# Two token blocks read by turns as TensorE's moving operand, in the expert scores and queries

## The reference, cut to what matters

```python
def peer_ffn(x, wq, sub_keys, u, v):
    q = jnp.einsum('bld,dk->blk', x, wq).reshape(b, L, PEER_HEADS, 2, PEER_HALF)
    s = jnp.einsum('blhpc,hpnc->blhpn', q, sub_keys)
    # two top-k steps choose eidx (which experts) and the gates g = softmax(top_s)
    def blk(inp):                       # one block of 128 tokens
        h = jnp.einsum('td,tkd->tk', xt, u[et])
        a = gt * jax.nn.gelu(h, approximate=False)
        return jnp.einsum('tk,tkd->td', a, v[et])
```

## Time and profile before

| | us |
|---|---|
| median of 3 executions | 3771.06 (3770.87 to 3773.51) |
| the profiled execution, its own time | 3770.78 |
| its span, first to last instruction | 3768.9 |
| TensorE busy in it | 3748.6 |
| VectorE busy | 2470.0 |
| ScalarE busy | 1904.0 |
| GpSimd busy | 974.0 |

### The profile page before, as it was taken

One profiled execution on the slowest core, in us unless ns is written; L12 is line 12 of the kernel. 1 busy time (PEld: TensorE's weight loads), 2 busy tenths in 40 slices (PEclk: granted clock), 3 DMA queues, 4 the chain that ended last, 5 costly groups with the idle time before them and its releaser, 6 DMA issues.

```text
span 3768.9 us, 58143 instructions
## 1 busy us (share of the span) xinstructions
PE 3748.6 (99%) x19216; PEld 3168.9 (84%) x19216; DVE 2470.0 (66%) x4281; ACT 1904.0 (51%) x2859; POOL 974.0 (26%) x557
## 2 busy tenths in 40 slices
PE   9999999999999999999999999999999999999998
PEld 7778888888888888888787788888888888888887
DVE  6766599985555555555687665999855555555556
ACT  4675455554444444444456654555544444444443
POOL 1000038777760000000011000477777600000000
PEclk9999999999999999999999999999999999999999
DMA  8665567777777666666666555677777776666664
GB/s 299 235 213 190 202 201 213 210 216 211 208 210 265 244 239 239 244 240 239 216 227 236 186 201 191 213 210 210 217 209 210 211 266 244 241 237 244 243 238 172
DMA packets 294652, 842.44 MB, mean 224 GB/s; under 512 B 98832, under 2 KB 198672, under 8 KB 210192
## 3 DMA queue, kind: packets, MB, share of 16 engines
q1 hardware_dynamic: 183952, 807.30, 61.0%
q0 software_dynamic: 73728, 0.29, 4.3%
q10 hardware_dynamic: 36864, 33.57, 2.8%
HBM read 771.57 MB, written 69.47 MB: 223 GB/s over the span
## 4 chain that ended last, share of the span: by engine, by line
PE 98%; DVE 1%; DMA 0%; ACT 0%; issue 0%; SPq 0%; DVEq 0%; ACTq 0%
PE bank L470 27%; PE bank L472 14%; PE bank L702 12%; PE bank L704 12%; PE bank L703 12%; PE bank L485 6%; PE bank L487 6%; PE bank L486 6%; PE bank L513 1%; PE bank L526 1%; PE bank L542 1%; PE bank L671 0%; PE bank L498 0%; DMA arena<-x_t_in 0%; PE bank L457 0%
## 5 line engine op out<-in xcount | busy, mean ns | idle before, releaser
L1143 DVE TENSOR_TENSOR lo<-raw,hi 128x1024 fp32r<-128x1024 f32 x1288 | 1583.8, 1231 | 1017.3 <-ACT hi L762 1008.1
L762 ACT ACTIVATE hi<-raw 128x1024 fp32r<-128x1024 f32 x1288 | 1362.6, 1059 | 1428.8 <-PE bank L704 748.4
L470 PE MATMUL bank<-xhl,hi 128*128 128x512 f32 x4480 | 1146.7, 393 | 0.0
L1109 POOL DMA_INDIRECT gates_scratch<-sel,slots x512 | 911.4, 1780 | 874.4 <-issue 484.5
L470 PEld LDWEIGHTS bank<-xhl,hi 128*128 128x128 f32 x4480 | 795.3, 189 | 131.8
L702 PE MATMUL bank<-hi,xhl 128*128 128x512 f32 x2016 | 784.6, 389 | 1.1 <-DVE xhl L1619 0.9
L704 PE MATMUL bank<-hi,xhl 128*128 128x512 f32 x2016 | 784.3, 389 | 0.0
L703 PE MATMUL bank<-lo,xhl 128*128 128x512 f32 x2016 | 784.3, 389 | 0.0
L472 PEld LDWEIGHTS bank<-xhl,lo 128*128 128x128 f32 x4480 | 630.9, 190 | 56.9
L472 PE MATMUL bank<-xhl,lo 128*128 128x256 f32 x4480 | 646.6, 282 | 0.0
L702 PEld LDWEIGHTS bank<-hi,xhl 128*128 128x128 f32 x2016 | 378.4, 188 | 80.7 <-DVE lo L1143 1.7
(11 more groups left out here) (177 smaller groups left out, 2070.0 us busy)
## 6 DMA issues: line engine op xcount, KB each, us to landing
raw<-u_t SPq DMA_DIRECT2D x256, 1024.0 KB
raw<-v_t SPq DMA_DIRECT2D x256, 1024.0 KB
raw<-w_in SPq DMA_DIRECT2D x76, 1024.0 KB, 4.9
gates_scratch<-arena SPq DMA_DIRECT2D x32, 1024.0 KB, 8.4
raw<-w_out SPq DMA_DIRECT2D x32, 1024.0 KB
raw<-wq SPq DMA_DIRECT2D x32, 1024.0 KB
gelu_scratch<-gelu_out ACTq DMA_DIRECT2D x256, 128.0 KB
scr<-gelu_scratch SPq DMA_DIRECT2D x256, 128.0 KB, 4.6
```

The source lines that it names most:

```text
L470: pe.matmul(acc[:], w, xhl[:, c, :, :].rearrange("p a t -> p (a t)"), start=(c == 0), stop=False)
L762: act.activation(to[:], half, ACT.Copy).then_inc(hi_done, 1)
L1109: pool.indirect_dma_start(out=gate_dram[layer].rearrange("i p t -> (i p t)").unsqueeze(1), out_offset=bass.IndirectOffsetOnAxis(ap=slots[: ...
L1143: dve.tensor_tensor(wide_lo[v][:], half, wide_hi[v][:].bitcast(F32), ALU.subtract).then_inc(lo_done, 1)
```

## The change

The moving operand of `both_parts` is read in another order, and the evictions of those banks undo it. Before, a matmul reads tokens 0, 1, 2, ... of a part. After, it reads token 0 of the first block, token 0 of the second (512 bytes further), token 1 of the first, and so on; in the 512-column matmul the high part is read so first and then the low part. So the PSUM columns come in the order "token, block". The writes to PSUM stay one after the other. The four evictions (L864, L1017 and VectorE's sums at L1463 and L1468) read the bank with a step of two elements and write `q_t` and `gelu_out` in the old order. No instruction is added, removed or moved on any engine.

```diff
+def by_block(cols):
+    return cols.rearrange("p (t b) -> p b t", b=NB)
+
+def in_blocks(cols):
+    return cols.rearrange("p (b t) -> p b t", b=NB)
...
                         for c, w in zip(chunks, wh):
-                            pe.matmul(acc[:], w, xhl[:, c, :, :].rearrange("p a t -> p (a t)"), start=(c == 0), stop=False)
+                            pe.matmul(acc[:], w, xhl[:, c, :, :].rearrange("p a (b t) -> p a t b", b=NB), start=(c == 0), stop=False)
                         for c, w in zip(chunks, wl):
-                            last = pe.matmul(acc[:, L:2 * L], w, xh[:, c, :], start=False, stop=(c == DC - 1))
+                            last = pe.matmul(acc[:, L:2 * L], w, xh[:, c, :].rearrange("p (b t) -> p t b", b=NB), start=False,
+                                             stop=(c == DC - 1))
...
-                            act.activation(q_t[:, 4 * g + j, :], bank[4 * (g % 2) + j][:, L:2 * L], ACT.Copy).then_inc(q_stored, 1)
+                            act.activation(in_blocks(q_t[:, 4 * g + j, :]), by_block(bank[4 * (g % 2) + j][:, L:2 * L]), ACT.Copy).then_inc(q_stored, 1)
...
-                        act.activation(gelu_out[m % 2][:], bank[m % 2][:, L:2 * L], ACT.Copy).then_inc(crossed, 1)
+                        act.activation(in_blocks(gelu_out[m % 2][:]), by_block(bank[m % 2][:, L:2 * L]), ACT.Copy).then_inc(crossed, 1)
...
-                            dve.tensor_tensor(q_t[:, 4 * g + j, :], bank[4 * (g % 2) + j][:, 0:L], q_t[:, 4 * g + j, :],
-                                              ALU.add).then_inc(q_summed, 1)
+                            total = in_blocks(q_t[:, 4 * g + j, :])
+                            dve.tensor_tensor(total, by_block(bank[4 * (g % 2) + j][:, 0:L]), total, ALU.add).then_inc(q_summed, 1)
...
-                        dve.tensor_tensor(gelu_out[m % 2][:], bank[m % 2][:, 0:L], gelu_out[m % 2][:], ALU.add).then_inc(summed, 1)
+                        total = in_blocks(gelu_out[m % 2][:])
+                        dve.tensor_tensor(total, by_block(bank[m % 2][:, 0:L]), total, ALU.add).then_inc(summed, 1)
```

## The result

The changed kernel takes 3722.31 us (3720.27 to 3723.70, 4 runs) against 3771.26 us before (3770.87 to 3773.51, 4 runs): ratio 0.987, 95% interval 0.985 to 0.989. It is 49 us faster, where 1434 us more were forecast.

The account below looks back on a forecast made before the run. TensorE's matmuls were taken to bound the kernel, so every nanosecond of theirs counts. The profiled 3770.8 us + 1434 for the moving operand + 0 for the evictions gave 5204.8, forecast 5205 us; whole range 3750 to 5340.

Parts of the forecast that it names:

- What bounds the kernel: Whole kernel: only the number of TensorE's matmuls and the time of each count; TensorE busy 3748.6 of 3768.9 us.
- Edit one, the moving operand: Scores and queries: the new read order costs one cycle more per column, 320 ns per pair, 1434 us in all.
- a picture of a port that fetches two neighbours: TensorE's moving read: neighbours fetched together, only one of two delivered when each element lies elsewhere, so the pace halves.
- half pace: Changed matmuls: 444 ns wide and 226 narrow, 5205 us, own range 5150 to 5340; the likeliest case, chance 0.38.
- a part of the price: Changed matmuls: only some elements pay, half a cycle per column, 717 us more, 4488 us; chance 0.12.
- The bound below: Changed matmuls: at best nothing or a little gain, 4480 x 4.5 = 20 us, from 231 against 226 ns.
- The sum for all of it: Changed matmuls: if the whole fixed part of both kinds (18 + 12 ns) went, 134 us less, 3637 us.
- the small gain: Scores' wide matmuls: reading from two places by turns saves 4.5 ns each, 20 us, giving 3751 us; chance 0.15.
- a conflict with other reads on the same memory: Scores: moving read conflicts with weight loads and ScalarE's and VectorE's writes, making 231 ns against 226; turns spread it.
- Edit two, the evictions: PSUM reads with a step of two: at most +198 ns for ScalarE and +261 for VectorE; taken as 0 us overall.
- The two rules of the Trainium skill: Moving read: one penalises a new 16-byte line at each access, so time rises; the other has one cycle per column, unchanged.

Follow-up runs that it names:

- e10: Against the kernel before: product with `v` made for only the first 64 tokens of each block, 64 stationary columns in place of 128; 3791.6 us.
- e1: Against the changed kernel: 128 blocks of 2 tokens in place of 2 of 128, so the moving operand is read with a step of 2 elements; 5251.8 us.
- e2: Against the changed kernel: 64 blocks of 4 tokens, a moving read with a step of 4 elements (16 bytes); 5316.3 us.
- e6: Against the changed kernel: 32 blocks of 8 tokens, a moving read with a step of 8 elements (32 bytes); 5113.4 us.
- e12: Against the changed kernel: turns inside groups of eight tokens, two places 16 bytes apart; 3719.6 us.
- e11: Against the changed kernel: turns inside groups of 128 tokens, two places 256 bytes apart; 3722.0 us.
- e4: Against the changed kernel: the product with `v` also reads its moving operand by turns from two halves, 1024 bytes apart; 3655.6 us.
- e13: Against the kernel before: in the product with `v` all 128 stationary columns are read from one element; 3797.7 us.
- e5: Against the changed kernel: 4 blocks of 64 tokens, four places 256 bytes apart read by turns; 4117.8 us.
- e16: Against the changed kernel: all moving weights read by turns 16 bytes apart, laid out to match; routing and scatters take the blocks by turns; 3601.14 us.
- e7: Against the changed kernel: turns inside each group of four tokens (0, 2, 1, 3), two places 8 bytes apart; 3770.6 us.

## Why the prediction was wrong

- *What bounds the kernel.* Right: TensorE's distance of starts, and in the runs that were a little slower each nanosecond of it counted (e10: 3.3 ns more for each of 6144 matmuls, 21 us more in all). When the pace was 6% quicker, the bound had moved in part.
- *Edit one, the moving operand.* Here it failed, at "one cycle more for each column, 768 x 0.417 = 320 ns for a pair". Measured: 22 ns less for a pair, so neither the size nor the sign was right. The step was taken from a picture of a port that fetches two neighbours and loses one of them if the next read lies elsewhere. e1, e2 and e6 show half pace (451, 461, 431 ns) for a steady step, and e12, e11 and the change itself none of it for two places in turn (216 ns). In the picture's own terms, what was fetched is not lost when the next read lies in one other place. The prediction named this as "the two streams are each in order and each keeps its own fetched neighbours for a while", under a part of the price, but did not follow it to its end.
- *The bound below* was too near. "If the reading order is what makes this 4 to 5 ns" took the gain from 231 against 226 ns, and held the remaining 13 ns for the matmul's own. 11 of those were the reading order as well, in the product with `v` too (e4). The sum for all of it stood there, 134 us, and was left outside the range.
- *The rivals.* The sign was the small gain's, with 0.15. Its mechanism, a conflict with other reads on the same memory, is not borne out for the 11 ns, since less to read for the weights takes nothing away (e10, e13); for the 4 ns between 231 and 227 it stays open. Its price, 20 us, was a fifth of the pace's 97.
- *Edit two, the evictions.* Right: 384 and 425 ns, unchanged.
- *What a faster TensorE would meet* was not asked, since a slower one was forecast. The row for it stood there: VectorE busy for 333 of 360 us in the routing leaves 7.5%, and a pace 6% quicker uses up nearly all of it. No row showed when the scatters end, and that they would lengthen could not be read from one trace.
- *The two rules of the Trainium skill.* Neither forecast a gain. The penalty for a new line at each access ("Advanced Engine Details and Errata", section "SBUF Cachelines") agrees with e2 and e6, 461 and 431 ns, and not with the change, where each read lies in another line than the one before and a matmul takes 216 ns. One column per cycle ("TensorE: Matmul & The Clock Gate", section "Step-by-step: what each phase is for"), taken as holding for any order, comes near the change (216 ns for 213), and not e1, e2, e5 and e6.

## What to carry to other kernels

Where float32r matmuls follow each other without waits, compare the distance of their starts with their columns at the granted clock: of a fixed 13 ns each, 11 go, 5% at 512 columns, if the moving operand is read by turns from two places 16 bytes or more apart, each moving to its neighbour; weights can be laid out in memory so that no eviction changes (e16). A steady step in the moving operand takes twice the time, and four places a third more than two, so of what was tried it is two or none. And when the bound engine gets quicker, look beforehand for what ends just ahead of it: here half of a 97 us gain went to VectorE's steps and to scatters that had ended 66 us before anything needed them.

## What the runs showed of the hardware that was not expected

- In a settled row, a float32r matmul with a contiguous moving operand has the next one start 227 ns later at 512 columns and 120 at 256, by turns of two 216 and 112, in steps of 8, 16 and 32 bytes 451, 461 and 431 (512 columns), by turns of four 283.
- Turns inside groups of four neighbours make no difference (e7: the distances of the kernel before, and 3770.6 us).
- With half of the weights to load, or one element for all, a wide matmul is 3 and 4 ns slower, not faster (e10, e13).
- GpSimd's scatters are longer in the runs in which TensorE and, with it, the other engines work faster: 1585 ns in the mean at half pace (e1), 1679 in e5, 1780 before, 1893 after. Whether the one causes the other was not tried.
- VectorE and ScalarE read 128 x 256 elements of PSUM in steps of two at the price of neighbours, 425 and 384 ns.
